# Keys of a paged cache fetched by indirect DMA of four pages at a time and transposed in 32x32 blocks by VectorE, in place of one page per DMA and transposes on TensorE

## What is computed

```python
k_sel = jnp.where(is_past, cache_k[phys, slot].astype(k.dtype), gather(k, nidx))
v_sel = jnp.where(is_past, cache_v[phys, slot].astype(v.dtype), gather(v, nidx))
...
logits = jnp.einsum('bthd,btkhd->bthk', q, k_sel).astype(jnp.float32) * ATT_SCALE
logits = logits + jnp.swapaxes(bias, -1, -2).astype(jnp.float32)
logits = jnp.where(valid[:, :, None, :], logits, -jnp.inf)
p = jax.nn.softmax(logits, axis=-1).astype(v_sel.dtype)
out = jnp.einsum('bthk,btkhd->bthd', p, v_sel)
```

## Time and profile before

| | us |
|---|---|
| median of three runs (lowest, highest) | 1597.6 (1593.25, 1598.45) |
| the profiled execution: its span | 1593.2 |
| what the lowest run has beside that span | 0.05 |
| TensorE matmul busy | 1471.7 |
| VectorE busy | 762.0 |
| ScalarE busy | 511.5 |
| GpSimd busy | 234.5 |

### The profile page before, as it was taken

One profiled execution on the slowest core, in us unless ns is written; L12 is line 12 of the kernel. 1 busy time (PEld: TensorE's weight loads), 2 busy tenths in 40 slices (PEclk: granted clock), 3 DMA queues, 4 the chain that ended last, 5 costly groups with the idle time before them and its releaser, 6 DMA issues.

```text
span 1593.2 us, 32571 instructions
## 1 busy us (share of the span) xinstructions
PE 1471.7 (92%) x13518; PEld 1334.5 (84%) x13518; DVE 762.0 (48%) x1030; ACT 511.5 (32%) x818; POOL 234.5 (15%) x371
## 2 busy tenths in 40 slices
PE   7999998979979989899998998899799999999995
PEld 4867798957867778797777998799699999999995
DVE  5288699496514540025540135543555555552123
ACT  4243223324323341023341122122344455442121
POOL 3423234154210000000000000321000110000000
PEclk8899999989999999999999999899799999999998
DMA  5415223122159979999869976133322233223221
GB/s 173 149 27 159 65 80 113 57 96 73 49 188 369 332 249 342 383 358 329 310 223 402 363 258 240 34 125 104 113 80 80 80 90 95 83 98 102 79 83 60
DMA packets 179278, 266.58 MB, mean 167 GB/s; under 512 B 20522, under 2 KB 136539, under 8 KB 178043
## 3 DMA queue, kind: packets, MB, share of 16 engines
q1 hardware_dynamic: 167947, 243.95, 44.5%
q0 software_dynamic: 5104, 11.11, 2.1%
q10 hardware_dynamic: 6080, 9.44, 1.6%
HBM read 240.28 MB, written 24.18 MB: 166 GB/s over the span
## 4 chain that ended last, share of the span: by engine, by line
PE 77%; DVE 8%; DMA 5%; ACT 3%; SPq 2%; issue 2%; POOL 2%; ACTq 0%; DVEq 0%
PE PS L987 14%; PE PS L989 13%; PE PS L988 13%; PE PS L1197 8%; PE PS L1210 4%; PE PS L1245 3%; PE PS L1319 3%; PE PS L1318 3%; PE PS L1317 3%; DMA R<-in_cache_v 3%; PE PS L1028 2%; PE PS L1029 2%; PE PS L1030 2%; PE PS L1173 1%; PE PS L1120 1%
## 5 line engine op out<-in xcount | busy, mean ns | idle before, releaser
L987 PE MATMUL PS<-xn_hi,WH 128*128 128x288 f32 (+1 forms) x1424 | 430.7, 302 | 16.0 <-DVE xn_lo L1614 13.2
L988 PE MATMUL PS<-xn_lo,WH 128*128 128x288 f32 (+1 forms) x1424 | 424.7, 298 | 0.0
L989 PE MATMUL PS<-xn_hi,WL 128*128 128x288 f32 (+1 forms) x1424 | 424.6, 298 | 0.0
L987 PEld LDWEIGHTS PS<-xn_hi,WH 128*128 128x128 f32 (+1 forms) x1424 | 271.1, 190 | 33.1 <-issue 22.2
L988 PEld LDWEIGHTS PS<-xn_lo,WH 128*128 128x128 f32 (+1 forms) x1424 | 271.9, 191 | 0.0
L989 PEld LDWEIGHTS PS<-xn_hi,WL 128*128 128x128 f32 (+1 forms) x1424 | 271.6, 191 | 0.0
L582 DVE TENSOR_TENSOR WL<-W,WH 128x2048 fp32r<-128x2048 f32 (+2 forms) x69 | 145.7, 2112 | 241.6 <-ACT WH L1358 241.6
L1358 ACT ACTIVATE WH<-W 128x2048 fp32r<-128x2048 f32 (+2 forms) x81 | 145.1, 1791 | 90.2 <-PE PS L1319 74.9
L1197 PE MATMUL PS<-CST,R 128*128 128x128 f32 x1024 | 142.7, 283 | 9.8 <-DMA R<-in_cache_k 9.5
L1793 DVE COPY RB<-PS 128x512 f32<-128x512 f32 x128 | 88.3, 691 | 115.7 <-PE PS L1197 115.7
L1197 PEld LDWEIGHTS PS<-CST,R 128*128 128x128 f32 x1024 | 112.1, 143 | 35.9 <-issue 25.7
(11 more groups left out here) (257 smaller groups left out, 2423.2 us busy)
## 6 DMA issues: line engine op xcount, KB each, us to landing
R<-in_cache_k SPq DMA_DIRECT2D x128, 512.0 KB, 5.3
R<-in_cache_v SPq DMA_DIRECT2D x128, 512.0 KB, 7.0
W<-in_w_in SPq DMA_DIRECT2D x30, 1024.0 KB, 5.4
W<-in_w_up SPq DMA_DIRECT2D x44, 512.0 KB, 4.6
W<-in_w_down SPq DMA_DIRECT2D x16, 704.0 KB, 4.4
x_scratch<-xT SPq DMA_DIRECT2D x2, 2304.0 KB, 9.0
W<-in_w_branch_a SPq DMA_DIRECT2D x4, 1024.0 KB, 7.9
W<-in_w_branch_b SPq DMA_DIRECT2D x4, 1024.0 KB, 6.1
```

What stands on the lines that cost most here:

```text
L987: pe.matmul(out, hi[:, k, cols], x.hi_block(n)[:, tokens], start=first, stop=False)
L988: pe.matmul(out, hi[:, k, cols], x.lo_block(n)[:, tokens], start=False, stop=False)
L989: return pe.matmul(out, lo[:, k, cols], x.hi_block(n)[:, tokens], start=False, stop=last)
```

## The change

The key stage works on four pages at once, page `kp` of the group's four sequences. GpSimd fetches them with one indirect DMA: partition 32 bb + lane of the tile gets four consecutive keys of sequence bb's page, 4 lane + r for r in 0 to 3, which is one row of 16 KB. The row numbers (page x 32 + lane) are made once at the start from the page table (`PROW`, `KROW`). Two such tiles of 2 MB (`KR`) take the place of the eight ring slots in the key stage. DVE transposes each tile in two instructions (halves u of four heads) in 32x32 blocks from SBUF to SBUF; since a partition holds keys 4 lane + r, its 32 outputs of a block are written four elements apart, so that the keys come out in order. There are three half-tile buffers (`KTB`). A partition then holds value d = 32 j + dd of key r, for its own sequence, and PE multiplies with queries laid out as blocks of 32 partitions (`QB`), adding j = 0 to 3 up: 32 matmuls of 32 stationary by 128 moving columns for four pages, as many as before. The transposes on PE and both their copies are gone. The logits use one bank where they used a pair.

Moved with it: `QB` is filled by ACT (32 small copies) in place of POOL's QZ; ACT, not SP, writes and reads back the mask; SP loads values alone and starts the first eight when the last key tiles are transposed. Side tiles: 2 at the start, 5 in each key stage, 2 in each softmax, 4 and 3 in the value stages, 1 at the end. The value accumulators and the logits take single banks, the side tiles both pairs.

```diff
-    two, three = {7: 1, 16: 1}, {4: 1, 10: 1, 16: 1}
-    SIDE_V = [two, two, two, three, two, two, three, {4: 1, 10: 1}]
+    SIDE_K = [2, 5, 8, 11, 14]
+    SIDE_V = [{8: 1}, {8: 1}, {8: 1}, {8: 1}, {8: 1}, {8: 1}, {8: 1}, {}]
...
-    put_side(('start',), 3)
+    put_side(('start',), 2)
     for G in range(2):
-        put_side(('softmax', G, 0), 1)
+        for kp in SIDE_K:
+            put_side(('K', G, kp), 1)
+        put_side(('softmax', G, 0), 2)
...
+        KR = [blocks(R1[:, 4096 * i:4096 * i + 4096], 4) for i in range(2)]
+        KTB = [a.rearrange("p (n k r) -> p n k r", n=16, r=4) for a in (RB[:, 0:2048], R3[:, 0:2048], R3[:, 2048:4096])]
...
-            G, kind, n = (seq - 8) // 128, (seq - 8) // 64 % 2, (seq - 8) % 64
-            if kind == 0:
-                e.wait_ge(single_filled, single.slots['kp', G, n, 1][0] + 1)
+            G, kind, n = seq // 128, seq // 64 % 2, seq % 64
+            if kind == 0 and n >= 8:
+                e.wait_ge(S_("k_transposed"), 32 * G + 2 * (n // 4 - 1))
+            elif kind == 0:
+                e.wait_ge(S_("v_pages_used"), 64 * G - 4 + 4 * (n // 4))
+            elif n < 8:
+                e.wait_ge(S_("k_transposed"), 32 * G + 30 + 2 * (n // 4))
             else:
-                e.wait_ge(S_("v_pages_used"), 64 * G + n + 1)
+                e.wait_ge(S_("v_pages_used"), 64 * G + n - 7)
...
+        def load_keys(e, G, kp):
+
+            page_freed(e, 128 * G + 4 * kp)
+            e.indirect_dma_start(out=R1[:, 4096 * (kp % 2):4096 * (kp % 2) + 4096], out_offset=None,
+                                 in_=cache_k[0].rearrange("n (k r) h d -> (n k) (r h d)", r=4),
+                                 in_offset=bass.IndirectOffsetOnAxis(ap=KROW[:, 16 * G + kp:16 * G + kp + 1], axis=0))\
+                .then_inc(key_in[kp % 2], 16)
...
+            pool.memset(QB, 0.0).then_inc(S_("queries_cleared"), 1)
+            load_keys(pool, 0, 0)
...
+            load_keys(pool, 0, 1)
...
+            for kp in range(2, NPAGES):
+                load_keys(pool, 0, kp)
...
-                        for u in range(2):
-                            claim(pe, 'kp', G, n, u)
-                            for i in range(4):
-                                h = 4 * u + i
-                                last = pe.transpose(bank('kp', G, n, u)[:, P * i:P * i + P],
-                                                    ring[seq % 8][:, HD * h:HD * h + HD], ident)
-                            done(last, 'kp', G, n, u)
...
+                    for u in range(2):
+                        pe.wait_ge(S_("k_transposed"), 32 * G + 2 * kp + u + 1)
+                        keys = KTB[(2 * kp + u) % 3]
+                        for j in range(4):
+                            for c in range(4):
+                                last = pe.matmul(bank('kl', G, kp)[32 * c:32 * c + 32, P * u:P * u + P],
+                                                 QB[:, G, 4 * u + c, j, :],
+                                                 keys[:, 4 * c + j, :, :].rearrange("p k r -> p (k r)"),
+                                                 start=(j == 0), stop=(j == 3))
...
+                    sides('K', G, kp)
...
+            act.wait_ge(S_("queries_cleared"), 1)
+            for G in range(2):
+                for bb in range(4):
+                    for j in range(4):
+                        t = TP + 32 * G + 8 * bb
+                        last = act.activation(QB[32 * bb:32 * bb + 32, G, :, j, 8 * bb:8 * bb + 8],
+                                              qT[32 * j:32 * j + 32, :, t:t + 8], ACT.Copy)
+            last.then_inc(S_("sample_queries"), 1)
+            act.wait_ge(S_("sample_mask"), 1)
+            act.dma_start(mask_scr, S).then_inc(S_("mask_out"), 16)
             sides('start')
+            act.wait_ge(S_("mask_out"), 16)
...
-                for n in range(64):
-                    filled(dve, 'kp', G, n, 1)
-                    dve.tensor_copy(KTb[n % 2][:, 4:8, :], blocks(bank('kp', G, n, 1), 4))\
-                        .then_inc(drains('kp', G, n, 1), 1)
...
+                        dve.transpose(KTB[n % 3].rearrange("p n k r -> p r n k"), KR[kp % 2][:, :, 512 * u:512 * u + 512]
+                                      .rearrange("p r (n d) -> p r n d", n=16))\
+                            .then_inc(S_("k_transposed"), 1)
+
+                for kp in range(NPAGES):
+                    transposed(kp)
+                    if kp >= 2:
+                        logits(kp - 2)
+                    if kp == 13:
                         drained(dve, 'kl', G, 11)
                         dve.tensor_reduce(EARLY, LS[:, :, 0:12 * P], AX_X, ALU.max)
+                    splits('K', G, kp)
```

More of the change, by code:

```diff
@@ L104, in shape_constants @@
     put('bucket', hot)
+    put('lane', np.tile((i % 32)[:, None], (1, 8)))
     return c
@@ L223, in hybrid_kernel @@
     for G in range(2):
-        for n in range(64):
-            single.add('kp', G, n, 0)
-            single.add('kp', G, n, 1)
         for kp in range(NPG):
-            pair.add('kl', G, kp, at=kp % 2)
-        for i, tile in enumerate(side_at['softmax', G, 0] + side_at['softmax', G, 1]):
-            pair.add(*tile, at=(i + 1) % 2)
+            single.add('kl', G, kp)
+            for tile in side_at.get(('K', G, kp), ()):
+                pair.add(*tile)
+        for tile in side_at['softmax', G, 0] + side_at['softmax', G, 1]:
+            pair.add(*tile)
         for g in range(2):
@@ L234, in hybrid_kernel @@
         for b in range(4):
-            pair.add('o', G, b, at=0)
+            single.add('o', G, b)
             for kp in range(NPG):
                 for tile in side_at.get(('V', G, b, kp), ()):
-                    pair.add(*tile, at=1)
+                    pair.add(*tile)
             single.add('ot', G, b, 0)
             single.add('ot', G, b, 1)
-    pair.add(*side[-1], at=1)
+    for tile in side_at['end',]:
+        pair.add(*tile)
     for c in range(8):
@@ L487, in hybrid_kernel @@
         idx_in = [[S_(f"idx_pages_in{a}_{i}") for i in range(4)] for a in range(2)]
+        key_in = [S_(f"key_tile_in{i}") for i in range(2)]
         page_in = [S_(f"page_in{i}") for i in range(8)]
@@ L822, in _ @@
                 idx_pages(pool, s, 1)
+            pool.wait_ge(S_("rows_in"), 64)
+            pool.wait_ge(S_("consts_in"), 16)
+            link(pool.tensor_copy(RB[:, 32:64], PROW[:, :]))
+            link(pool.tensor_scalar(RB[:, 32:64], RB[:, 32:64], 32.0, const('lane')[:, 0:1], ALU.mult, ALU.add))
+            link(pool.tensor_copy(KROW[:, :], RB[:, 32:64]))
             drained(pool, 'bias', H - 1)
@@ L919, in _ @@
                 pool.dma_start(MG[32 * j:32 * j + 32, :], mask_scr[32:64, :]).then_inc(S_("mask_in1"), 16)
+            for kp in range(NPAGES):
+                load_keys(pool, 1, kp)
             pool.wait_ge(S_("ws_in"), 16)
@@ new lines, in _ @@
+                for kp in range(NPAGES):
+                    if (G, kp) == (0, 0):
+                        pe.wait_ge(S_("sample_queries"), 1)
+                    claim(pe, 'kl', G, kp)
+                    for u in range(2):
[7 more added lines that the diff above has]
+                                                 start=(j == 0), stop=(j == 3))
+                        if u == 0:
+                            last.then_inc(S_("k_half_used"), 1)
+                        else:
```

113 lines of the change are left out of this document (52 added, 61 removed).

## The result

The changed kernel takes 1645.0 us (median of 4 runs, 1640.38 to 1647.92), the kernel before 1595.4 us beside it (4 runs, 1592.35 to 1598.45): a ratio of 1.0307, 95% interval 1.0278 to 1.0335. It is slower by 3%. One of ten executions of a later kernel (`e2_dense_write_read`) took 3247 us, twice its other nine, and the ratios leave it out. The profiled execution has a span of 1645.6 us, 52.4 us more than the 1593.2 of before.

What follows compares the result with a forecast made beforehand. It took PE to bound the key stages, and PE's side tiles with DMA the value stages. Its stage terms ended the attention at 884.4 instead of 930.0, saving 45.6 us: 1552 us beside 1597.6, forecast 1530 to 1580, all cases 1528 to 1690.

Steps and rivals of the forecast that it cites:

- I take 2.3 us, one step a column: Key stages: price of each of 64 DVE transpositions of 128x2048, taken from DVE's 2048-column subtraction at 2.29 us.
- The rival that I had given 0.43: Key stages: step-of-four write costs DVE a second step, 4.4 us a transposition, 1661 us in all; chance 0.43.
- its mild form: Key stages: smaller extra cost of the step-of-four write, kernel near 1600 us; chance 0.12 within the 0.43.
- its full one: Key stages: transposition of 4.4 us, DVE needing 162 us a stage, kernel at 1661 us.
- the break-even of 3.5 us: Key stages: transposition price at which DVE's time eats the whole gain, 23 us more in each of two stages.
- its formula: DVE's time in a key stage: 32 transpositions plus 20.8 us of other work, 162 us at 4.4 us each.
- the prediction's own line for 3.7 us: Whole kernel: with transpositions between 3.3 and 3.7 us it is where it was, about 1590 to 1605 us.
- my sum: Sample attention: start, key, softmax and value stages and a gap added up, ending at 884.4 against 930.0 before.
- The loop: Key stages: two-tile round of issue, landing and transposing, 12.5 us for two steps; 6.9 a step with additions, 109.5 a stage.
- The value stages: Value stages: 32.7 and 31.9 MB at DMA's pace of 390 GB/s, side tiles covered, 84 and 82 us.
- The start: Before the first key stage: first gather issued at about 447.5, first transposition at about 455.5.
- the gap: Between first value stage and second key stage: wait for the first key tile, asked for after value page 60; 7 us.

Runs made afterwards that it cites:

- e2_dense_write_read: Changed kernel with the transposition writing in runs and PE reading in runs, DVE reordering the permuted logits from PSUM; 1598.9 us, ratio 1.0032 to the kernel before the change.

## Why the prediction was wrong

**The step that failed: "I take 2.3 us, one step a column".** It is the price of the operation without what the change does to it. Written in runs the transposition costs 2.29 us, and written with the step of four 3.84 (3.7 each, two in a row). The rival that I had given 0.43, DVE as the bound, came true, between its mild form and its full one: above the break-even of 3.5 us that I had worked out, below 4.4. With 3.7 us its formula gives 32 x 3.7 + 20.8 = 139 us of DVE; it is 135.7 and 133.0. Two stages of 139 for 109.5 us would have made 1611 us by that sum (the prediction's own line for 3.7 us says 1605), not 1645: the price is the largest of the misses, not the only one. With the write in runs, at my price, the kernel takes 1599 us and is still outside my 1530 to 1580. In the profile of its counterpart with the step of two (1598.9 us) the attention ends 47 us later than my sum: 19 of them lie in the key stages, 21 in the value stages, the rest in the start and the softmax. I chose by the nearest row in engine and shape, and no row of before writes with a step at all: for the one property that was new, the rows were silent, so the nearness of that row was no ground for making it the likeliest case.

**The loop.** "= 12.5 us for two steps, 6.3 us a step" was some 2 us short for the gather: 9.5 us in the mean, not 7.9; no run splits it into issue, index reading (for which my 0.5 us was an allowance) and data. In the changed kernel DVE hides most of this. With the write's price gone it shows: stages of 122.6 and 115.1 us where I had 109.5. I took the 1.9 us of a small load for the fixed part and 420 GB/s for the rest; in the changed kernel, in windows of 2 us from the release at 497.5, the engines move 98, 234, 414 and 429 GB/s, then 150:

```profile
497.50:499.50 2.00, 2.00 (x64) 1.60 (x64) 2.00 (x2) 0.65 (x1) 0.94 (x1) 1.00 0.53 98
499.50:501.50 2.00, 0.03 (x2) 0.00 (x0) 2.00 (x2) 0.00 (x0) 0.00 (x0) 1.00 0.60 234
...
505.50:507.70 2.20, 1.69 (x32) 1.15 (x24) 0.09 (x1) 0.00 (x0) 0.91 (x1) 0.50 0.64 150
```

The full rate holds for less than half of the time.

**The value stages.** "so it is DMA's pace: at 390 GB/s 84 and 82 us" was 15.5 and 9.0 us short. Five tiles fewer than before in the first and six in the second took only 10.6 us off each. The ring does not cover a side tile that falls among pages paced by DMA; taken out, the stages are 79.9 and 80.6 us. My own rule would have given 29.4 MB at 390 GB/s, 75 us, for such a stage, so some 5 us in each are not the tiles'. I had warned of the lower clock in the key stage only.

**The start** came at 460.5, not at 455.5: ahead of the first transposition on DVE stands its part of a weight's split, which waits for ACT until 458.27.

```profile
447.81 7.42 ACT L1528 ACTIVATE R<-R 32x64 f32<-32x64 f32 x28 [1.95 <-POOL R L919]
...
456.32 1.92 ACT L1375 ACTIVATE WH<-W 128x2048 fp32r<-128x2048 f32 x1
...
458.27 2.29 DVE L593 TENSOR_TENSOR WL<-W,WH 128x2048 fp32r<-128x2048 f32 x1 [22.14 <-ACT WH L1375]
```

I had named the work that the change puts on ACT there, 32 small copies, and not who waits behind ACT. The rows show them back to back from 447.8 to 456.3 us, and the rounding that DVE waits for right behind; in the kernel before ACT began one at 444.87. No run moved the copies.

**What held:** the softmax stages, 19.2 and 18.5 us for 18.4 and 18.5; the gap, 5.8 for 7; the products, hidden at the lower clock but for 2.5 us; and that what is behind the attention keeps its length. With the step of two, half gathers and the tiles moved, all three mis-sized terms mended, the kernel is at 1556.8 us beside the 1552 that I had forecast for the change as it was. That is partly luck: its key stages take 117.7 and 114.0 us, not 109.5, with seven tiles that I had in the value stages. The break-even did not hold for the kernel: it was to be at 3.5 us, and at 2.29 us the kernel is only level with before.

## What to carry to other kernels

Price a new instruction with its access pattern, not by its count of elements: a write in steps of 16 bytes made this one 1.6 to 1.7 times as long, while steps of 8 bytes cost at most 6% (2.43 us for 2.29) and needed only the instruction cut in two. With two buffers, add up the whole loop (release, issue, landing, use) and halve it; if the landing is the long part, cut the buffer into pieces that are freed and asked for by themselves, rather than look for a faster load. And when a change frees an engine in one stage, look for work elsewhere that stands in the way of a transfer and move it there: that was worth 27 us here, and it pays with the slow write too (1627 against 1645 us).

## What the runs showed of the hardware

An indirect DMA of 128 rows of 16 KB took 8.3 to 11.5 us from release to landing where it stood on the chain of the changed kernel; of 8 KB rows, with others under way, 7.4 to 10.2 us, and 15.4 once. POOL's issue took 0.95 and 0.97 us in the mean. Direct loads to 32 partitions each, four for a tile, kept the DMA engines at 1.00 busy with 225 GB/s. Products that read 128 columns with a step of 32 elements had a mean of 408 ns against 350 in runs. And 1 MB of weights, loaded beside the gathers, landed in 10.8 us (median of two) in the first key stage of the changed kernel and in 28.4 us, a single load, beside the half gathers, against 5.6 us in the median over the kernel:

```profile
W<-in_w_in SPq DMA_DIRECT2D x2, 1024.0 KB, 10.8
```

```profile
W<-in_w_in SPq DMA_DIRECT2D x1, 1024.0 KB, 28.4
```
